# Two heads' scores and values issued in turn on the two halves of TensorE's array, and the masked part of causal attention left out

## The reference

```python
# first block, every layer: bidirectional attention, 8 query heads over 2 key/value heads, head size 64
def attend(q, k, v):
    s = jnp.einsum("bqhgd,bkhd->bhgqk", q, k).astype(jnp.float32) * ATTN_HEAD_DIM ** -0.5
    p = jax.nn.softmax(s, axis=-1).astype(v.dtype)
    return jnp.einsum("bhgqk,bkhd->bqhgd", p, v)
...
# second block, every layer: three mixers of 8 score heads each, all causal, 256 tokens
    a_out = merge_heads(rms_norm(diff_attention(...), diff_g) * (1.0 - lambda_init))
    b_out = merge_heads(stick_breaking_attention(...))
    c_out = merge_heads(moba_attention(...))
    merged = (jax.nn.sigmoid(g_diff) * (a_out @ w_diff_o)
              + jax.nn.sigmoid(g_sb) * (b_out @ w_sb_o)
              + jax.nn.sigmoid(g_moba) * (c_out @ w_moba_o))
```

## Time and profile before

| what | value |
|---|---|
| median of three runs | 3744.45 us (3739.84 to 3749.76) |
| profiled execution, its own time | 3740.8 us |
| span of its instructions | 3739.0 us |
| TensorE matmuls busy | 3566.2 us, 95% of the span |
| DVE, ACT busy | 1622.8 us, 663.3 us |
| attention of block 1 | about 503 to 573 us (layer 0), 1665 to 1712 us (layer 1) |
| mixers of block 2 | about 2481 to 2618 us (layer 0), and as long again about 850 us later |

### The profile page before, as it was taken

How to read it: one execution, slowest core, us unless ns; L and a number is a source line. 1 busy time by engine, 2 the same in 40 slices (tenths; PEclk the granted TensorE clock), 3 DMA queues, 4 the chain that set the end, 5 groups by cost and what they waited for, 6 DMA issues and landing times.

```text
span 3739.0 us, 48543 instructions
## 1 busy us (share of the span) xinstructions
PE 3566.2 (95%) x19318; PEld 2829.6 (76%) x19318; DVE 1622.8 (43%) x3291; ACT 663.3 (18%) x1524; POOL 361.7 (10%) x276
## 2 busy tenths in 40 slices
PE   7999999999999999989998999999999899999998
PEld 3444754444888875767898999887799898877898
DVE  0164371113555113452178475034476673134574
ACT  2111341001221011232022111113210111123110
POOL 0000000002443300000077300000000000000000
PEclk8999999999999999999999999999999999999999
DMA  5134001221223423502444444332344344432343
GB/s 210 68 134 170 34 1 59 87 79 68 90 81 108 149 96 122 221 17 95 164 148 140 148 169 164 135 118 85 113 170 165 130 167 144 141 113 91 131 168 120
DMA packets 66556, 449.98 MB, mean 120 GB/s; under 512 B 7200, under 2 KB 10272, under 8 KB 17824
## 3 DMA queue, kind: packets, MB, share of 16 engines
q1 hardware_dynamic: 66336, 446.95, 34.5%
HBM read 445.87 MB, written 1.05 MB: 120 GB/s over the span
## 4 chain that ended last, share of the span: by engine, by line
PE 89%; DVE 6%; issue 2%; ACT 2%; DMA 1%; SPq 0%; DVEq 0%; ACTq 0%
PE bank L836 38%; PE bank L1081 36%; PE bank L1214 3%; PE bank L1291 2%; DVE region_b L2297 2%; PE bank L884 1%; PE bank L1061 1%; PE bank L1326 1%; PE bank L902 1%; PE bank L972 1%; PE bank L1039 1%; PE bank L997 1%; PE bank L924 1%; DMA residual<-in_x 1%; PE bank L1050 1%
## 5 line engine op out<-in xcount | busy, mean ns | idle before, releaser
L836 PE MATMUL bank<-normed,weight_ring 128*128 128x256 f32 (+1 forms) x3520 | 1045.5, 453 | 10.0 <-ACT normed L1470 6.3
L836 PEld LDWEIGHTS bank<-normed,weight_ring 128*128 128x128 f32 x3520 | 664.1, 191 | 363.5 <-issue 301.9
L1081 PE MATMUL bank<-normed,weight_ring 128*128 128x128 f32 (+1 forms) x3872 | 524.1, 294 | 32.4 <-issue 18.2
L1081 PEld LDWEIGHTS bank<-normed,weight_ring 128*128 128x128 f32 x3872 | 496.0, 196 | 50.0 <-issue 24.4
L1081 PE MATMUL bank<-normed,mixer_small 128*128 128x128 f32 (+1 forms) x2464 | 315.0, 282 | 0.0
L1081 PEld LDWEIGHTS bank<-normed,mixer_small 128*128 128x128 f32 x2464 | 297.8, 192 | 4.5
L1081 PE MATMUL bank<-region_a,weight_ring 128*128 128x128 f32 (+1 forms) x1936 | 258.6, 291 | 9.1 <-DVE region_a L2307 9.1
L1081 PEld LDWEIGHTS bank<-region_a,weight_ring 128*128 128x128 f32 x1936 | 242.6, 193 | 22.4 <-DVE region_a L2307 9.3
L2651 POOL TENSOR_TENSOR mixer_small<-weight_ring 128x512 f32<-128x512 f32 (+1 forms) x68 | 91.1, 1340 | 1729.3 <-DMA weight_ring<-w_up 1456.6
L836 PE MATMUL bank<-region_a,weight_ring 128*128 128x256 f32 (+1 forms) x768 | 210.2, 433 | 0.0
L836 PEld LDWEIGHTS bank<-region_a,weight_ring 128*128 128x128 f32 x768 | 145.8, 190 | 61.0 <-issue 46.3
(11 more groups left out here) (263 smaller groups left out, 3854.3 us busy)
## 6 DMA issues: line engine op xcount, KB each, us to landing
weight_ring<-w_ada SPq DMA_DIRECT2D x48, 1024.0 KB, 5.2
weight_ring<-w_up SPq DMA_DIRECT2D x44, 1024.0 KB, 4.8
weight_ring<-w_f1up SPq DMA_DIRECT2D x44, 1024.0 KB, 4.8
weight_ring<-w_f2up SPq DMA_DIRECT2D x44, 1024.0 KB, 4.8
weight_ring<-w_mg SPq DMA_DIRECT2D x32, 768.0 KB, 4.2
weight_ring<-w_qk SPq DMA_DIRECT2D x24, 1024.0 KB, 4.8
weight_ring<-w_gt SPq DMA_DIRECT2D x24, 1024.0 KB, 4.8
weight_ring<-w_v SPq DMA_DIRECT2D x20, 1024.0 KB, 4.9
```

Source lines behind the costliest of these rows:

```text
L836: mm = nc.tensor.matmul(out_ap, tile(b, t0 + k), src[:, k0 + k, c0:c1], start=first and k == 0, stop=last and k == kn - 1)
L1081: mm = nc.tensor.matmul(out_ap, lhs(k), rhs(k), start=start and k == 0, stop=stop and k == n - 1)
```

## The change

Block 1: a job is now a pair of heads (z = 0 and 1) for one query half q. Its scores are one matmul of each head, on the upper and the lower half of the rows. The values of both heads of a pair are issued once, after the second job of the pair, with the heads in turn for each key tile, on the left and right half of the columns. The output unit is taken in odd steps. Block 2: scores of heads n+2 and n+3 are issued together in even steps, the heads in turn; for softmax heads the first 128 queries have only 128 keys, so scores, mask, maxima, exponentials and normalisation work on 384 columns instead of 512, and the maxima are two reductions. Values of both heads are issued together in odd steps, the heads in turn.

```diff
@@ attention_jobs, make_plan
-    jobs = [(X0, NT, i, z) for i in range(4) for z in range(2)]
+    jobs = [(X0, NT, i, q) for i in range(4) for q in range(2)]
...
+            if n >= 0 and n % 2:
+                plan.take_units(f"ao{l}.{n // 2}", 1)
             if 0 <= n + 1 < len(jobs):
                 plan.take_units(f"at{l}.{n + 1}", 2)
-            if n >= 0 and n % 2 == 0:
-                plan.take_units(f"ao{l}.{n // 2}", 1)
...
-            if n + 2 < 24:
-                plan.take_at(f"s2.{n + 2}", n % 2)
+            if n + 2 < 24 and n % 2 == 0:
+                plan.take_at(f"s2.{n + 2}", 0)
+                plan.take_at(f"s2.{n + 3}", 1)
@@ attention1, TensorE
                 def scores(n):
-                    q0, keys, i, z = jobs[n]
-                    for q, u in enumerate(plan.units[f"as{l}.{n}"]):
+                    q0, keys, i, q = jobs[n]
+                    for u in plan.units[f"as{l}.{n}"]:
                         begin(u)
+                    for z, u in enumerate(plan.units[f"as{l}.{n}"]):
...
                     for k in range(keys // P):
-                        mm = nc.tensor.matmul(bank[u.bank][z * DH:(z + 1) * DH, 0:SEQ], va[:, k, z * DH:(z + 1) * DH],
-                                              apt[:, n % 2, k, :], start=k == 0, stop=k == keys // P - 1)
-                    if n % 2:
-                        mm.then_inc(bank_full[u.bank], 1)
-                    else:
-                        mm.then_inc(apt_half, 1)
+                        for z in range(2):
+                            mm = nc.tensor.matmul(bank[u.bank][z * DH:(z + 1) * DH, 0:SEQ], va[:, k, z * DH:(z + 1) * DH],
+                                                  apt[:, z, k, :], start=k == 0, stop=k == keys // P - 1)
+                    mm.then_inc(bank_full[u.bank], 1)
...
-                    if n >= 0:
+                    if n >= 0 and n % 2:
                         values(n)
@@ layer2, TensorE
+                    units = [plan.units[f"s2.{n + z}"][0] for z in range(2)]
+                    for u in units:
+                        begin(u, 0, l)
                     if n < 16:
...
+                        parts = [(tq, slice(0, P), tk, slice(0, P), slice(0, P)), (tq, slice(P, SEQ), tk, slice(0, SEQ), slice(P, W3))]
                     else:
...
+                        parts = [(tk, slice(0, P), tq, slice(0, SEQ), slice(0, SEQ)), (tk, slice(P, SEQ), tq, slice(P, SEQ), slice(SEQ, W3))]
+                    for x, (ta, a, tb, b, o) in enumerate(parts):
+                        for z, u in enumerate(units):
+                            mm = nc.tensor.matmul(bank[u.bank][:, o], qk2[z * DH:(z + 1) * DH, ta, a],
+                                                  qk2[z * DH:(z + 1) * DH, tb, b], start=True, stop=True)
+                            if x:
+                                mm.then_inc(bank_full[u.bank], 1)
...
+                        heads = [(slice(z * DH, (z + 1) * DH), slice(base + z * DH, base + (z + 1) * DH), z) for z in range(2)]
+                    for rows, cols, z in heads:
+                        nc.tensor.matmul(bank[u.bank][rows, 0:SEQ], vt2[:, 0, cols], pt2[:, z, 0:SEQ], start=True, stop=False)
+                    for rows, cols, z in heads:
+                        mm = nc.tensor.matmul(bank[u.bank][rows, P:SEQ], vt2[:, 1, cols], pt2[:, z, SEQ:W3],
+                                              start=False, stop=True)
+                    mm.then_inc(bank_full[u.bank], 1)
...
-                    if n + 2 < 24:
+                    if n + 2 < 24 and n % 2 == 0:
                         scores(n + 2)
@@ layer2, DVE
-                        v.tensor_reduce(nmax[:, n % 4, :], s, AX.X, ALU.max, negate=True).then_inc(amax_ready, 1)
+                        step(v.tensor_reduce(nmax[:, n % 4, 0:1], s[:, 0:P], AX.X, ALU.max, negate=True))
+                        v.tensor_reduce(nmax[:, n % 4, 1:2], s[:, P:W3], AX.X, ALU.max, negate=True).then_inc(amax_ready, 1)
```

More of the change, by code:

```diff
@@ L160, in constants @@
     k = np.arange(SEQ)
-    put("causal", np.concatenate([np.where(k[None, :] > (i + P * q)[:, None], -BIG, 0.0) for q in range(2)], axis=1))
+    put("causal", np.concatenate([np.where(k[None, :P * (q + 1)] > (i + P * q)[:, None], -BIG, 0.0) for q in range(2)], axis=1))
     put("upto", (i[:, None] >= i[None, :]).astype(np.float32))
@@ L440, in attention_jobs @@
 def attention_jobs(l):
-    jobs = [(X0, NT, i, z) for i in range(4) for z in range(2)]
+    jobs = [(X0, NT, i, q) for i in range(4) for q in range(2)]
     if l < DEPTH - 1:
-        jobs += [(0, CTX, i, z) for i in range(4) for z in range(2)]
+        jobs += [(0, CTX, i, q) for i in range(4) for q in range(2)]
     return jobs
@@ L1363, in values @@
                     else:
[L1364 removed]
+                        pe.wait_ge(apt_ready, T.next(apt_ready, 2))
                     if n < 8:
[L1366 removed]
+                        heads = [(slice(0, P), slice((n // 2) * P, (n // 2 + 1) * P), n % 2)]
                     else:
[L1368 to L1379 removed]
+                        base = (8 if n < 16 else 4) * P + (n - 1) % 8 * DH
+                        heads = [(slice(z * DH, (z + 1) * DH), slice(base + z * DH, base + (z + 1) * DH), z) for z in range(2)]
[5 more added lines that the diff above has]
+                    mm.then_inc(bank_full[u.bank], 1)
                 for n in range(-2, 24):
                     g = gate_tile(n)
[L1383 removed]
+                    if n + 2 < 24 and n % 2 == 0:
                         scores(n + 2)
@@ L1551, in copies @@
                 def copies(n):
-                    _, keys, _, _ = jobs[n]
+                    _, keys, _, q = jobs[n]
                     if n >= 2 and n % 2 == 0:
-                        act.wait_ge(apt_half, A.next(apt_half))
-                    if n >= 2 and n % 2:
-                        full_bank(plan.units[f"ao{l}.{(n - 2) // 2}"][0])
-                    for q, u in enumerate(plan.units[f"at{l}.{n}"]):
+                        full_bank(plan.units[f"ao{l}.{n // 2 - 1}"][0])
+                    for z, u in enumerate(plan.units[f"at{l}.{n}"]):
                         full_bank(u)
-                        a_(apt[:, n % 2, 0:keys // P, q * P:(q + 1) * P],
+                        a_(apt[:, z, 0:keys // P, q * P:(q + 1) * P],
                            bank[u.bank][:, 0:keys].rearrange("p (k c) -> p k c", c=P), ACT.Copy
@@ L1567, in attention1 @@
                         copies(n + 1)
-                A.next(apt_half)
             def conv_norm(l, c0, n):
@@ L1783, in exps @@
                         act.wait_ge(amax_ready, A.next(amax_ready))
-                        for q in range(2):
-                            a_(pr2[:, n % 4, q, :], sm2[:, n % 4, q, :], ACT.Exp, bias=nmax[:, n % 4, q:q + 1],
+                        for q, x in enumerate((slice(0, P), slice(P, W3))):
+                            a_(pr2[:, n % 4, x], sm2[:, n % 4, x], ACT.Exp, bias=nmax[:, n % 4, q:q + 1],
                                accum_out=asum[:, n % 4, q:q + 1]).then_inc(aexp_ready, 1)
@@ L2552, in finish @@
                             own(step(v.tensor_scalar(r, r, lam, None, ALU.mult)))
-                            for q in range(2):
-                                last = step(v.tensor_scalar(x[:, q, :], x[:, q, :], r[:, q:q + 1], None, ALU.mult))
+                            for q, t in enumerate(tiles_):
+                                last = step(v.tensor_scalar(x[:, t], x[:, t], r[:, q:q + 1], None, ALU.mult))
                             own(last)
-                            y, r0 = pr2[:, (n - 1) % 4], asum[:, (n - 1) % 4, :]
-                            for q in range(2):
-                                ins = v.scalar_tensor_tensor(x[:, q, :], y[:, q, :], r0[:, q:q + 1], x[:, q, :],
-                                                             ALU.mult, ALU.add)
+                            y, r0 = pr2[:, (n - 1) % 4, :], asum[:, (n - 1) % 4, :]
+                            for q, t in enumerate(tiles_):
+                                ins = v.scalar_tensor_tensor(x[:, t], y[:, t], r0[:, q:q + 1], x[:, t], ALU.mult, ALU.add)
                                 if q == 0:
```

76 lines of the change are left out of this document (21 added, 55 removed).

## The result

The changed kernel takes **3704.49 us** (median of 4 runs, 3694.6 to 3711.89); the kernel before, timed beside it, 3742.69 us (3739.84 to 3749.76). The ratio is 0.9893, 95% interval 0.9865 to 0.9922. It is faster by 38 us, where the forecast said 50. The forecast's own ratio, 3694 to 3744.45, is 0.9865 and lies on the edge of that interval, so that by the times alone the forecast and the result can hardly be told apart; what was off in its sum is read from the traces.

What follows compares the result with a forecast made beforehand. TensorE, busy 95% of the span, was taken as the bound, with a DVE and ACT loop limiting block 1. Block 2's 34.4 us plus block 1's 16.0 made 50.4 off the 3744.45 median: 3694 us, range 3684 to 3704.

Steps and rivals of the forecast that it cites:

- Overlap of halves: Both blocks: matmuls on two row halves or two column halves overlap fully, 0.65 us per block 2 value pair.
- Rival 1: Both blocks: overlap falls one pass short everywhere, costing 7.5 us in block 2 and 2 in block 1: 3704; chance 0.12.
- Rival 2: Scores of both blocks: halves issued in turn do not overlap, 14.3 us and 2 in block 1: 3710; chance 0.08.
- Rival 6: Both blocks: turns cost a layout change each and nothing overlaps, so the kernel is slower: 3760; chance 0.02.
- Rival 3: Block 2: new waits as TensorE arrives too early at pairs' transposes, 19 us: 3713; chance 0.04.
- the two forecast waits: Block 2, transposes of steps 11 and 13: TensorE waits for DVE about 1.1 us each, 2.2 us a layer lost.
- Block 2, 17.2 us a layer: Block 2's mixers: scores, values and fewer layout changes save 19.4 us a layer, 17.2 after waits, 34.4 for both.
- Behind block 2's steps, 0 us: Work after block 2's last steps: no change; savings in steps 20 to 23 are lost to DVE's and ACT's chain.
- Rival 4: Block 1's attention: the clock stays at half throughout, 16 us lost instead of 16 gained: 3726; chance 0.05.
- Block 1, 16.0 us: Block 1's attention: 8.5 us gained in layer 0 and 7.5 in layer 1, 16.0 together.
- The loop: Block 1's attention: DVE and ACT waiting on each other set the period, about 4.17 us a 512-key job, from 4.80.
- Rival 5: Block 1's attention: TensorE stays the bound, so 36 us are gained instead of 16: 3674; chance 0.04.

Runs made afterwards that it cites:

- experiment 4: Changed kernel with both heads of each pair on the same half of the array, values head by head, so no overlap possible: 3741.57 us, ratio 0.9997.
- Experiment 3: Changed kernel with each pair's matmuls issued one head after the other instead of in turn, in both blocks: 3703.08 us, ratio 0.9887.
- experiment 6: Changed kernel with DVE's rescaling of block 2's differential heads put behind the next head's normalising and the following scores: 3697.63 us, ratio 0.9879.
- experiment 1: Changed kernel with block 2 put back as before, so only block 1's attention is changed: 3723.91 us, ratio 0.9950.
- experiment 2: Changed kernel with block 1 put back as before, so only block 2's mixers are changed: 3717.36 us, ratio 0.9923.
- experiment 7: Changed kernel with two gate tiles a layer computed within block 2's steps instead of ahead of them: 3688.75 us, ratio 0.9860.
- experiment 5: Changed kernel with DVE taking the first of the two maxima of each block 1 job twice: 3720.32 us, ratio 0.9942.
- experiment 12: Changed kernel with the edits of experiment 6 and experiment 7 together: 3684.47 us, ratio 0.9853.
- experiment 8: Changed kernel with the transposes of odd jobs of block 1 done twice: 3697.63 us, ratio 0.9878.
- experiment 11: Changed kernel with the edits of experiment 6, experiment 7 and experiment 8 together: 3677.20 us, ratio 0.9819.

## Why the prediction was right, and where its sum was off

The forecast of 3694 us (3682 to 3712) was on the right side and 10 us too low. By its own steps:

- **Overlap of halves: right.** The rows had it, the changed profile has it in every pair, and experiment 4 took it away and lost the whole gain. Rivals 1, 2 and 6 fall. Rival 3 falls too: the idle time of a stage of block 2, 8.1 us, is the two forecast waits (2.3) and the three of the tail (5.8). Experiment 3 shows that for groups of four passes to a half even the turns are not needed.
- **Block 2, 17.2 us a layer: right, 16.7.** The 17.2 held up to the last gate product (122.7 us before, 105.2 after: 17.5). The two waits of 1.1 us came as 1.16, ended by DVE; experiment 6 removed both by moving the rescaling. The tail, forecast as unchanged, went from 14.17 to 14.95 us, through the clock.
- **Behind block 2's steps, 0 us: wrong, 5.8 lost.** The prediction said that what is saved in the tail is lost. It was lost and cost more: idle time in the tail grew from 3.3 to 5.8 us, the clock fell to half in its last stretch, and the weight products that follow ran at half clock for some 4 us in each layer, which accounts for some 2 us a layer; the rest of the 3.1 and 2.7 lies further on. Experiments 1 and 2 put the 5.8 in block 2's part, experiment 7 took most of it away by filling the tail. Rival 4 had this mechanism, but only for block 1.
- **Block 1, 16.0 us: mis-sized, 13.4.** The loop is right: 4.08 a job where 4.17 was forecast, 2.77 with 256 keys where it was 2.78, TensorE idle behind ACT's and DVE's parts, and experiment 5's extra reduction shows in full. Rival 5 falls. What failed is the clock: each stage had rounds of values at half speed that the sum had at full speed (in layer 0 3.59 us for 1.95 and 1.57 for 1.08, in layer 1 3.63 and 3.29 for 1.95), with mean clocks of 0.89 and 0.83 (0.93 and 0.89 before). In experiments 7 and 12, where these rounds kept the full clock, the stages gained 9.1 and 8.7 us, beyond the forecast 8.5 and 7.5. So rival 4 was true in part, at 2.2 us a layer where it was priced at 32 for both. How much of it an execution meets is chance as far as is known: five traces with this same code in block 1 (the changed kernel, 1, 6, 7 and 12) have 60.8 to 63.5 us in layer 0 and 38.5 to 40.7 in layer 1.
- **The rest: 2.9 us in one stretch** that the change does not touch. In the ten traces with equal code there, it takes 765 to 776 us. The rows below the table show where the difference comes from: DVE instructions of the feed-forward convolution that meet work of GpSimd, and not the clock. Experiments 1 (765.2) and 2 (775.9) lie on either side of before (769.3) and after (772.2), so it is no sign of the change, though the change may shift when the two engines meet.

Together: 50.4 forecast, less 0.9 in block 2's stages, 2.6 in block 1, 5.8 behind block 2, 2.2 elsewhere, gives 38.9, and the spans differ by 39.0. That the sum closes is for this one execution; the runs of the changed kernel spread over 17 us, and another one would have split off other amounts for the clock and for that stretch.

## What to carry to other kernels

When a change takes TensorE work out of a stage, ask where its idle time now lies and what runs right behind it: a tail that was 3 us idle and became 6 cost another 3 us a layer in work behind it that was never edited, and filling it with work from elsewhere took about 14 us off block 2 and what follows it in the profiled executions. In a loop of two half-busy engines the share of busy time does not show the bound; measure the period between two equal instructions that wait only for each other, and expect it as the new floor. Before a queue's order is changed to open such a loop, follow the ring of waits through every engine: here the new order closed a longer one. And before a few microseconds between two traces are put down to a change, compare a stretch with equal code: here one such stretch moved by up to 11 us.

## What the runs showed of the hardware

- Matmuls on the other half of the array begin ahead of earlier ones that are still queued on the first: 8 passes, four and four, take the same 0.93 us in turn or not, but 16, eight and eight, take 2.83 us against 1.95. The reach in this case is about four passes.
- Dense work after a tail with 5.8 us of idle time, in three waits of 1.4 to 2.5 us, started at half clock (0.53 over 7 us), after one with 3.3 us at full clock (1.00).
- A DVE instruction with two inputs of 128x255 (L2279) takes 0.47 us with GpSimd idle and mostly 1.2 to 1.5, at most 1.57, with GpSimd at work throughout.
- Work thrown away, in idle time of TensorE, did not slow the kernel (experiment 8). The runs of experiment 11, with it, spread over 3.5 us (five runs), those of experiment 12, without it, over 13 (four); that the one caused the other is not shown.
